# Four chunks of RWKV keys ahead of the first gram instead of eight, the rest in later steps

## The reference

```python
c = cp[:, :-2] * conv[0] + cp[:, 1:-1] * conv[1] + cp[:, 2:] * conv[2]
r, k, v, wd, ad, gd = split_last(c.astype(f32), RWKV_SIZES)
decay = jnp.exp(-jnp.exp(w_log))
a = jax.nn.sigmoid(a0[:, None, None] + jnp.einsum('btl,dlc->dbtc', ad, a_up))
kk = heads(k * k_k)
kk = kk / jnp.maximum(jnp.linalg.norm(kk, axis=-1, keepdims=True), 1e-12)
kd = heads(k * (1.0 + (a - 1.0) * k_a))
def step(S, inp):
    wt, kkt, kat, kt, vt, rt = inp
    S = (S * wt[..., None, :]
         - jnp.einsum('...vk,...k->...v', S, kkt)[..., :, None] * kat[..., None, :]
         + vt[..., :, None] * kt[..., None, :])
    return S, jnp.einsum('...vk,...k->...v', S, rt)
```

## Time and profile before

| | us |
|---|---|
| median of 3 executions | 1659.9 (1656.05 to 1661.16) |
| profiled execution, its own time | 1657.29 |
| span of the profiled execution | 1655.5 |
| TensorE busy | 1594.0 (96%) |
| VectorE busy | 802.1 (48%) |
| ScalarE busy | 738.1 (45%) |
| GpSimd busy | 754.3 (46%) |

### The profile page before, as it was taken

One profiled execution on the slowest core, in us unless ns is written; L12 is line 12 of the kernel. 1 busy time (PEld: TensorE's weight loads), 2 busy tenths in 40 slices (PEclk: granted clock), 3 DMA queues, 4 the chain that ended last, 5 costly groups with the idle time before them and its releaser, 6 DMA issues.

```text
span 1655.5 us, 31835 instructions
## 1 busy us (share of the span) xinstructions
PE 1594.0 (96%) x13137; PEld 1313.3 (79%) x13137; DVE 802.1 (48%) x1305; ACT 738.1 (45%) x1400; POOL 754.3 (46%) x676
## 2 busy tenths in 40 slices
PE   7999999999996999999999999999999999999998
PEld 6888888777774777778898877888888888888886
DVE  5104888527457765544513658443343334344336
ACT  5324888643665534424444754223323323322325
POOL 4221666221336634435464016547556555554651
PEclk9999999999998999999999999999999999999999
DMA  6110000221000010017233002012112111111203
GB/s 211 52 45 31 1 1 1 71 66 42 14 6 27 5 55 5 23 65 258 85 122 95 1 26 95 26 51 77 41 37 77 58 40 56 64 39 51 77 0 127
DMA packets 62734, 92.08 MB, mean 56 GB/s; under 512 B 4450, under 2 KB 45568, under 8 KB 62336
## 3 DMA queue, kind: packets, MB, share of 16 engines
q1 hardware_dynamic: 61728, 88.13, 16.3%
q0 software_dynamic: 864, 1.93, 0.5%
HBM read 82.70 MB, written 6.29 MB: 54 GB/s over the span
## 4 chain that ended last, share of the span: by engine, by line
PE 88%; DVE 6%; ACT 3%; issue 2%; DMA 1%; POOL 1%; SPq 0%; DVEq 0%; ACTq 0%
PE PS L2920 8%; PE PS L2921 8%; PE PS L2922 8%; PE PS L2481 7%; PE PS L2187 5%; PE PS L2190 5%; PE PS L2188 5%; PE PS L2927 5%; PE PS L2929 5%; PE PS L2928 5%; PE PS L2202 4%; PE PS L2204 4%; PE PS L2203 4%; PE PS L2286 3%; PE PS L2330 3%; PE PS L2558 2%
## 5 line engine op out<-in xcount | busy, mean ns | idle before, releaser
L640 POOL TENSOR_TENSOR WL<-RAW,WH 128x512 fp32r<-128x512 f32 x116 | 164.0, 1424 | 369.4 <-ACT WH L934 369.0
L2187 PE MATMUL PS<-HH,WH 128*128 128x512 f32 x416 | 165.2, 397 | 0.3 <-DVE SM L1566 0.3
L2132 DVE TENSOR_TENSOR X<-PS,X 128x512 f32<-128x512 f32 x160 | 110.5, 692 | 109.2 <-PE PS L2929 109.2
L840 POOL TENSOR_TENSOR WL<-WU_RAW,WH 128x512 fp32r<-128x512 f32 x60 | 77.1, 1292 | 188.1 <-ACT WH L917 188.1
L2188 PE MATMUL PS<-HL,WH 128*128 128x512 f32 x416 | 162.1, 390 | 0.0
L2927 PE MATMUL PS<-WH,FH 128*128 128x512 f32 x352 | 137.0, 389 | 1.7 <-DVE FL L2086 1.7
L2929 PE MATMUL PS<-WH,FL 128*128 128x512 f32 x352 | 136.9, 389 | 0.0
L2928 PE MATMUL PS<-WL,FH 128*128 128x512 f32 x352 | 136.9, 389 | 0.0
L2190 PE MATMUL PS<-HH,WL 128*128 128x512 f32 x416 | 133.5, 390 | 0.0
L934 ACT ACTIVATE WH<-RAW 128x512 fp32r<-128x512 f32 x117 | 71.5, 629 | 130.3 <-PE PS L2190 49.2
L2920 PE MATMUL PS<-HH,WH 128*128 128x512 f32 x320 | 124.5, 389 | 0.0
(11 more groups left out here) (419 smaller groups left out, 3871.0 us busy)
## 6 DMA issues: line engine op xcount, KB each, us to landing
WD_RAW<-in_ffn_w_down SPq DMA_DIRECT2D x44, 256.0 KB, 2.6
RAW<-in_w_in SPq DMA_DIRECT2D x43, 256.0 KB, 2.8
WG_RAW<-in_ffn_w_gu SPq DMA_DIRECT2D x20, 512.0 KB, 4.4
WU_RAW<-in_ffn_w_gu SPq DMA_DIRECT2D x20, 512.0 KB, 4.5
RAW<-in_w_out SPq DMA_DIRECT2D x28, 256.0 KB, 2.9
XT<-in_x SPq DMA_DIRECT2D x8, 512.0 KB, 6.5
X<-in_x SPq DMA_DIRECT2D x8, 512.0 KB, 5.9
RAW<-in_x_wq SPq DMA_DIRECT2D x16, 256.0 KB, 2.7
```

What stands on the lines that cost most here:

```text
L640: pool.tensor_tensor(w_low, raw_at(p), w_high.bitcast(F32), ALU.subtract).then_inc(w_lo, 2 if p < N_VAL else 1)
L840: pool.tensor_tensor(w_low, quarter(kind, i, name), w_high.bitcast(F32), ALU.subtract).then_inc(w_lo, 1)
L2187: pe.matmul(where(ct, i), wh[:, k, c], ah(kt)[:, t0:t0 + n], start=first and starts(ct, i), stop=False, skip_group_check=True)
```

## The change

VectorE prepares the first direction's keys in three parts instead of two halves: chunks 0 to 3, 4 to 7 and 8 to 15. Part 0 of first_keys and r_keys comes ahead of gram 0 (now both counted in r_pre, 4 in all), part 1 of both in step 0, first_keys part 2 in step 1, r_keys part 2 in steps 2 and 3, there behind inverse 3. The small strided copies of the keys' first columns leave VectorE; ScalarE does all of them in one instruction (128 x 32). On ScalarE the first key factor goes behind the first TMPV copy. The preparation of the second direction is spread anew: VectorE's scans from A, B, C of step 1 and A of step 2 to A and D of both; GpSimd's pieces from 3, 4, 4, 4, 1 to 3, 2, 4, 4, 3 in steps 0 to 4. Gram 2 waits for part 1, gram 4 for part 2.

```diff
-        DVE_PREP = {1: "ABC", 2: "A", 3: "ABCD", 4: "ABCD", 5: "D", 6: "ABCD", 7: "ABC"}
-        POOL_PREP = {0: (0, 0, 3), 1: (0, 1, 3), 2: (0, 1, 3), 3: (0, 1, 3), 4: (0, 1, 0)}
+        DVE_PREP = {1: "AD", 2: "AD", 3: "ABCD", 4: "ABCD", 5: "D", 6: "ABCD", 7: "ABC"}
+        POOL_PREP = {0: (0, 0, 3), 1: (0, 1, 1), 2: (0, 1, 3), 3: (0, 1, 3), 4: (0, 1, 2)}
...
                     act.wait_ge(r_conv, 6)
-                    key_factor(0, 0)
                     for ct in range(2):
                         act.activation(TMPV[:, ct, 1:T], PS[:, 2 * ct:2 * ct + 2, :].rearrange("p b t -> p (b t)")[:, 0:T - 1], ACT.Identity,
                                        scale=col(PTC_CONV + CONV[6 + ct])).then_inc(job_evac, 2)
-                    key_factor(1, 0)
+                        key_factor(ct, 0)
+                    act.activation(KR[:, 0, :, :, 0], KK[:, :, 0:T:C], ACT.Copy)
                     continue
...
-            def r_keys(ct, half):
-
-                c = slice(8 * half, 8 * half + 8)
+            PARTS = (slice(0, 4), slice(4, 8), slice(8, 16))
+
+            def r_keys(ct, part):
+
+                c, half = PARTS[part], part // 2
                 dve.wait_ge(r_kd, 2 * half + ct + 1)
                 dve.wait_ge(r_exp, 3 + ct)
                 link(TT(BKt[:, 1, ct, c], row(KS, ct)[:, c], BKt[:, 0, ct, c], ALU.mult))
-                TT(BKt[:, 0, ct, c], row(S3_, ct)[:, c], BKt[:, 0, ct, c], ALU.mult).then_inc(r_kd_used, 1)
-
-            def first_keys(ct, half):
-                c = slice(8 * half, 8 * half + 8)
+                TT(BKt[:, 0, ct, c], row(S3_, ct)[:, c], BKt[:, 0, ct, c], ALU.mult).then_inc(r_kd_used if part else r_pre, 1)
+
+            def first_keys(ct, part):
+                c = PARTS[part]
                 dve.wait_ge(r_exp, ct + 1)
-                dve.tensor_copy(KR[:, 0, ct, c, 0], KK[:, ct, 512 * half:512 * half + 512:C])
...
-                if p == 0:
-                    first_keys(0, 1)
+                if p < 2:
+                    first_keys(0, p + 1)
+                    first_keys(1, p + 1)
...
                 if p == 0:
-                    first_keys(1, 1)
-                elif p < 3:
-                    r_keys(p - 1, 1)
+                    r_keys(0, 1)
+                    r_keys(1, 1)
                 more_inputs(p, "C")
                 if mid:
                     inverse(mid, 3)
+                if p in (2, 3):
+                    r_keys(p - 2, 2)
                 if old:
                     results(old)
...
-            pe.wait_ge(r_pre, 2)
-            pe.wait_ge(r_kd_used, 2)
+            pe.wait_ge(r_pre, 4)
             pe.wait_ge(mix_moved, 48)
...
+                if j.g == 2:
+                    pe.wait_ge(r_pre, 6)
+                    pe.wait_ge(r_kd_used, 2)
                 if j.g == NT // 2:
-                    pe.wait_ge(r_pre, 4)
+                    pe.wait_ge(r_pre, 8)
                     pe.wait_ge(r_kd_used, 4)
```

## The result

| | before | changed |
|---|---|---|
| median, 6 executions each | 1657.99 us (1656.05 to 1661.16) | 1663.68 us (1661.47 to 1665.84) |
| ratio, 95% interval | | 1.0036 (1.0024 to 1.0049) |
| span of the profiled execution | 1655.5 | 1661.2 |
| mean granted clock, profiled execution | 0.995 | 0.992 |
| mean granted clock, mean of all executions | 0.9931 (91, from all the runs below) | 0.9907 (6) |

The clock runs at one of two levels, 1.0 (2.4 GHz) and 0.50 (1.2 GHz), so a mean of c over a span s means 2 x (1 - c) x s at the low one: 22.9 us per execution before, 31.0 in the changed kernel. I call this the cold time. It is a rough figure: the clocks are recorded to a thousandth, which is 3.3 us of it for one execution. In the two profiled executions the formula gives 16.6 and 26.6 us, while the stretches at 0.50 add up to 13.6 and 23.8.

A forecast was written before the change was run, and what follows sets the result against it. TensorE was taken to bound the kernel (88% of the chain), so only its waits around the first grams could move. Terms -0.35 + 0.25 - 1.65 + 0.9 + 0.6 = -0.25 us, from 1658.6 to 1658.4; range 1653.9 to 1663.2.

The forecast's parts named there:

- D: Predicted shift of VectorE's gram of step 4, behind which everything on TensorE should move equally: -0.25 us.
- Up to gram 0: Projections' end to gram 0: keys end 3.0 us sooner, but the MIX<-OW transfer's landing leaves 0.35 gained (0.2 to 0.5).
- Rival C: Before gram 0: the transfer does not hold it, TensorE's value turn ends last; gain 1.35, D -1.25, 1657.4 us; chance 0.1.
- What a product costs beside GpSimd: Steps 0 to 3: VectorE and GpSimd products take turns, each costing the GpSimd instruction ahead too, 0.6 to about 1.05 us.
- step 0: Four small first_keys products between system and inverse 0 make inverse 0 0.9 us late; +0.25 reaches gram 1 (0 to 0.7).
- Step 1: Four products ahead of inverse 2, fewer instructions before inverse 3: TensorE starts the next step sooner, -1.65 us (-2.6 to -0.4).
- the clock is a side term: After TensorE's idle stretch, 527 to 530: the clock falls again; a sooner rise is worth up to 1 us, counted nothing.
- if step 1 costs TensorE no less than before: One of three signs, named beforehand, that the prediction is wrong; it had TensorE gain 1.65 us there.
- Step 2: r_keys(0) behind inverse 3 costs 1.3 us, a moved scan delays inverse 1 and the coupling: +0.9 us (+0.2 to +1.9).
- Step 3: r_keys(1) newly between inverse 3 and results, where VectorE is the bound: +0.6 us beyond the preceding 0.9 (0 to +1.7).
- Rival B: Late r_keys between inverse 3 and results cost 2.5 us per pair, not 1.3: D +3.0, 1661.6 us; chance 0.2.
- Rival A: Steps 1 to 3: turns with GpSimd seldom bite and the clock rises early, -0.7: D -2.7, 1655.9 us; chance 0.2.

The follow-up runs named there:

- the gate's experiment: Changed kernel with TensorE's wait for the landing of MIX<-OW (mix_moved 48) ahead of gram 1 instead of gram 0: ratio 1.0016 to the kernel before.
- r_keys early: Changed kernel with r_keys for chunks 8 to 15 ahead of inverse 3 in steps 2 and 3: ratio 1.0021; with three matmuls in step 1's wait also, 0.9989.
- the last two runs: Seven extra matmuls ahead of the second direction's inputs: on the changed kernel with three matmuls, early r_keys, moved MIX<-OW wait, 0.9971; on the mended kernel before, 0.9984.

## Why the prediction was wrong

My sum was D = -0.25, 1658.4, with a range up to 1663.2, and "slower" at 0.06. (By its own rule, 2 us above the highest case of 1661.6, the range ends at 1663.6.) Measured 1663.68, ratio 1.0036: slower, and the whole interval above 1. By its steps:

1. *Up to gram 0, -0.35:* right. From 12.74 to 12.46 us after the projections' end, -0.28. The keys ended 9.96 after it (12.64 before), 2.7 sooner where I had 3.0. That the landing of MIX<-OW would be late next was right, and the gate's experiment shows it. Rival C falls.
2. *What a product costs beside GpSimd, and step 0, +0.25:* right. The four small products took 1.49, 0.83, 1.48 and 1.37 (0.41 to 0.42 in the quiet). inverse 0 stood at 521.11; my 520.4, with the 1.0 of the later projections added and the 0.3 gained ahead of gram 0 taken off, is 521.1. TensorE waited 1.35 for it. Gram 1 was 0.1 later than before, so 0.4 was lost behind the 0.3 gained. The rule of the Trainium skill ("SBUF — State Buffer", "Who interferes with whom"), that the second of two such instructions blocks until the first is done, agrees with these rows: GpSimd's own products ran 515.78 to 517.23, 518.06 to 519.51 and 519.47 to 520.91, and each of the three long ones here ended 0.3 us behind one of them.
3. *Step 1, -1.65:* **this is the step that failed**, by the sentence on the clock: "the clock is a side term ... whether it rises sooner is worth up to 1 us either way, and I take nothing". VectorE did as forecast: its four products took 3.7 us and inverse 2 ended at 531.2. The clock fell as forecast. But in the profiled execution it did not come back for 17 us, and TensorE's work in steps 1 and 2 took up to 1.8 times as long (gram 2 1.96, gram 3 1.10). Step 1 took 14.2 us, where 14.1 before less 1.65 was 12.5. That was one of my own signs of being wrong: "if step 1 costs TensorE no less than before". With the wait filled it takes 11.7, so VectorE's side of the term was there. But only 0.9 of that is the moved work: the kernel before with its wait filled takes 12.6, and the other 1.5 is what its own low clock cost.
4. *Step 2, +0.9:* right at full clock, where it took 12.0 and 12.1 us against 11.2. In the changed kernel it took 15.9; 3.8 to 3.9 of that is the clock, in the profiled execution.
5. *Step 3, +0.6:* mis-sized. It is +1.8 to +1.9 at full clock (13.1, 13.2). The r_keys pair itself cost 1.8, at the top of what I wrote; what I left out is that VectorE's other products of this step get longer beside GpSimd: the first pair took 1.80 (1.39 before) and the next product 1.79 (1.03). The second L1800 was shorter (0.78, L1799 1.45 before), as I had allowed for, so these products cost 0.5 in all. That GpSimd's later pieces are the reason is read from the rows; no run tests it. r_keys early takes only 0.5 off step 3. And step 4 is not free, as I had it ("Behind step 4 all is TensorE's and moves by D"): it took 11.6 us, and 11.4 with the wait filled, against 10.9.
6. *Rival B* asked for the full price of the late r_keys, 2.5, in both steps and got it in neither: 0.68 and 0.69 in step 2, 0.68 and 1.16 in step 3. That it said "slower" is luck, since its reason didn't come. *Rival A* said that the clock could help; it did the reverse.

The rows of VectorE's timeline behind point 5, before and changed:

```profile
551.96 1.39 DVE L1796 TENSOR_TENSOR KR<-KR,CIN 128x504 f32<-128x504 f32 x2
554.94 1.03 DVE L1799 TENSOR_TENSOR KR<-KR,KK 128x512 f32<-128x512 f32 x1
```

```profile
558.83 1.80 DVE L1797 TENSOR_TENSOR KR<-KR,CIN 128x504 f32<-128x504 f32 x2
561.21 1.79 DVE L1800 TENSOR_TENSOR KR<-KR,KK 128x512 f32<-128x512 f32 x1
```

How the measured loss divides, over all executions: the changed kernel has 8.1 us more cold time than the kernel before (31.0 against 22.9), which can cost 4.05 us at most, half of it, of a loss of 4.8 (means, 1663.9 against 1659.1) to 6.0 (ratio). Two runs beside each other say it more directly. With three matmuls in the wait of each (and the gate moved in the kernel before), the kernels have much the same cold time (16.9 and 16.0), and the changed one is still slower by 0.0016, 2.7 us (0.9998 against 0.9982; medians 1659.41 and 1656.44). So of the 0.0036 about 0.0020, 3.3 us, goes with the clock, and 2.7 us are the longer steps. The profiled steps at full clock give the same as an estimate: -0.3 up to gram 0, +0.4 in step 0, -0.9 in step 1, +0.8 in step 2, +1.9 in step 3 and +0.5 in step 4, +2.4 where my sum was -0.25. Each ratio is uncertain by about 0.0012, so the division is "half and half", no finer.

Two things stay open. In single executions the low stretches lie at other places (in the profiled one with r_keys early at 521 to 526, 532 to 539 and 559 to 563, in steps 0, 1 and 3), and the one around gram 0, which begins between 500 and 504, lasted 7 us in seven profiled executions, 10 in one and 14 in four, though only the last two runs, which are not among these, put work ahead of it. So the share of each step is known for the profiled executions only. And why the clock stayed low for 17 us in the changed kernel and for 7 in the kernel before, with much the same work behind the wait, no run here tells.

## What to carry to other kernels

A wait of a few microseconds on TensorE is not priced by its length. Ahead of a dense stretch its price is the length plus what the low clock costs behind it, so a forecast that moves such a wait must put a number on the granted clock of the stretch that follows, from the kernel's own windows, as a term and not as a remark; here it was 3.8 us in the profiled step 2 and about 3.3 of 6 over all executions. And a wait that was over a moment before another one ended stands in no view: list every semaphore of the instruction, and when each was full, before counting a gain at it.

## What the runs showed of the hardware that I had not expected

- The clock stayed at 0.50 for 17 us (531.0 to 548.0), with TensorE busy without a gap for the last 14 of them, while in the kernel before it rose at 537.4, with TensorE back at work from 533.8, and at 510.1, with TensorE at work from 505.3. It also fell there at 530.6, where TensorE's gaps since 520 had been 0.72 us at most.
- A float32 matmul of 128 x 128 by 512 columns occupies TensorE for 0.87 us at 2.4 GHz (11 in 9.6 us, recorded as 22), the decay inputs of 64 rows (64 x 128 by 512 columns, 4 in 1.99 us, recorded as 8) 0.50 each.
- Work that computes nothing made both kernels faster: -0.38% on the changed one, -0.18% on the kernel before (this with the gate moved, which had nothing to give there).
- Less cold time is not always less time: 13.2 us at 1654.7, and 10.2 at 1656.4, in the profiled execution with a low stretch behind gram 0 instead of ahead of it.
